# More gathered rows at the places of the second group's trunk, with three row buffers and whole weight blocks as they were

## The reference: what is computed

```python
x = x + merged @ w_mix_out       # the trunk: conv branch and GLA branch, gated and merged
x = x + _peer(_rmsnorm(x, norm2_g), peer_wq, peer_k1, peer_k2, peer_u, peer_v)
...
# in _peer, for each token: 8 heads of 16 experts each, of 16384
act = jax.nn.gelu(jnp.einsum('tkd,td->tk', u_tab[eb], hb))
return jnp.einsum('tk,tkd->td', gb * act, v_tab[eb])
```

## Time and profile before

| | |
|---|---|
| median of 3 runs | 4727.87 us (4722.62 to 4731.08) |
| the profiled execution | 4727.94 us, span 4725.9 us |
| PE busy | 4620.5 us (98%) |
| DVE busy | 2704.7 us (57%) |
| ACT, POOL busy | 542.8 us (11%), 904.6 us (19%) |
| data moved | 1352.17 MB, mean 286 GB/s |
| mean granted TensorE clock | 0.994 |

### The profile page before, as it was taken

The page is one execution under the profiler, slowest core; times in us unless marked ns, Lnnn a source line. Parts: engine busy times, 40 slices in busy tenths (PEclk is TensorE's granted clock), DMA queues, the critical chain, the costliest instruction groups (busy, mean ns, idle before and its releaser), DMA issues.

```text
span 4725.9 us, 47015 instructions
## 1 busy us (share of the span) xinstructions
PE 4620.5 (98%) x18646; PEld 3348.4 (71%) x18646; DVE 2704.7 (57%) x4672; ACT 542.8 (11%) x1255; POOL 904.6 (19%) x691
## 2 busy tenths in 40 slices
PE   8999999999999999999999999999999999999997
PEld 7888888888767567666667778888888844444443
DVE  4433500028567676645555459876878755555556
ACT  2111200011111101110000111112222200000000
POOL 1000000000111212023333232222333222222221
PEclk9999999999999999999999999999999999999999
DMA  4333444544667768568888789998998899999998
GB/s 176 142 136 140 159 152 145 209 177 154 215 229 256 298 222 308 200 234 347 350 338 352 278 342 341 342 332 330 359 348 333 335 395 412 412 383 411 417 411 326
DMA packets 239438, 1352.17 MB, mean 286 GB/s; under 512 B 43361, under 2 KB 43617, under 8 KB 133362
## 3 DMA queue, kind: packets, MB, share of 16 engines
q1 hardware_dynamic: 145362, 665.97, 37.9%
q0 software_dynamic: 93856, 683.19, 37.0%
HBM read 1308.38 MB, written 40.16 MB: 285 GB/s over the span
## 4 chain that ended last, share of the span: by engine, by line
PE 73%; DMA 19%; DVE 5%; issue 2%; ACT 0%; POOL 0%; POOLq 0%; DVEq 0%; ACTq 0%
PE ps L360 37%; PE ps L637 16%; PE ps L558 5%; PE ps L501 5%; DMA RING<-in_peer_v,table 4%; DMA RING<-in_peer_v,X 4%; DMA RING<-in_peer_u,X 4%; DMA RA<-in_uT 3%; DMA RING<-in_peer_u,table 3%; DVE CUR L857 2%; DVE RING L851 2%; PE pm L405 1%; PE ps L456 1%; PE pm L449 1%; PE ps L564 1%
## 5 line engine op out<-in xcount | busy, mean ns | idle before, releaser
L360 PE MATMUL ps<-X,BIG 128*128 128x320 f32 (+1 forms) x5632 | 1397.6, 410 | 6.9 <-DVE BIG L1242 6.4
L360 PEld LDWEIGHTS ps<-X,BIG 128*128 128x128 f32 x5632 | 1068.9, 190 | 319.0 <-issue 16.2
L857 DVE SCALAR_TENSOR_TENSOR CUR<-RING,wexp,CUR 128x2048 f32<-128x2048 f32 x320 | 752.0, 2350 | 398.2 <-DMA RING<-in_peer_v,table 283.4
L851 DVE CUSTOM_DVE_ANT_0 RING<-RING,CUR 128x2048 f32<-128x2048 f32 x320 | 730.3, 2289 | 405.5 <-DMA RING<-in_peer_u,table 276.0
L637 PE MATMUL ps<-X,RA 128*128 128x256 f32 x4096 | 903.6, 380 | 19.7 <-DMA RA<-in_uT 19.4
L637 PEld LDWEIGHTS ps<-X,RA 128*128 128x128 f32 x4096 | 773.4, 191 | 130.8 <-DMA RA<-in_uT 25.9
L1873 POOL DMA_INDIRECT RING<-in_peer_u,table x256 | 372.5, 1455 | 1364.0 <-DVE hidden L851 977.5
L1873 POOL DMA_INDIRECT RING<-in_peer_v,table x256 | 370.1, 1446 | 968.5 <-DVE CUR L857 754.6
L656 PE MATMUL ps<-RA,BIG 128*128 128x512 f32 x1024 | 492.2, 604 | 27.6 <-DMA RA<-in_peer_v 25.5
L656 PE MATMUL pm<-RA,BIG 128*128 128x512 f32 x1024 | 482.1, 594 | 1.3 <-DVE BIG L1352 1.3
L656 PEld LDWEIGHTS ps<-RA,BIG 128*128 128x128 f32 x1024 | 189.4, 191 | 295.2 <-issue 195.5
(11 more groups left out here) (293 smaller groups left out, 2886.4 us busy)
## 6 DMA issues: line engine op xcount, KB each, us to landing
BIG<-in_w_in_b SPq DMA_DIRECT2D x64, 2048.0 KB, 9.3
RA<-in_uT SPq DMA_DIRECT2D x256, 512.0 KB
RA<-in_peer_v SPq DMA_DIRECT2D x256, 512.0 KB
BIG<-in_w_gb_b SPq DMA_DIRECT2D x16, 2048.0 KB, 8.8
BIG<-in_w_ga_b SPq DMA_DIRECT2D x16, 2048.0 KB, 8.1
BIG<-in_w_gla_o_b SPq DMA_DIRECT2D x16, 2048.0 KB, 9.7
BIG<-in_w_mix_b SPq DMA_DIRECT2D x16, 2048.0 KB, 9.4
BIG<-in_w_q_b SPq DMA_DIRECT2D x16, 2048.0 KB, 9.1
```

The source lines that it names most:

```text
L360: last = pe.matmul(bank[:, 0:n], w[:, k, j * P:(j + 1) * P], src[:, k, 0:n], start=(k == 0), stop=(k == kt - 1))
L851: row_used.on(dve.tensor_tensor_reduce(out=row, in0=row, in1=h2cur[0:n, :], scale=1.0, scalar=0.0, op0=ALU.mult, op1=ALU.add, accum_out=hi ...
L857: row_used.on(dve.scalar_tensor_tensor(out=cur[0:n, :], in0=row, scalar=wexp[0:n, par, k:k + 1], in1=cur[0:n, :], op0=ALU.mult, op1=ALU.ad ...
```

## The change

Only numbers of the schedule change: how many gathered rows stand at each place of group 1's trunk.

```diff
-                    if g and tap in (5, 10, 15, 25):
+                    if g and tap in (3, 7, 11, 15, 25):
...
-                    spare((h, "z"), 4.8)
+                    spare((h, "z"), 7.2)
...
-                    spare((h, "kq"), 24.0)
+                    spare((h, "kq"), 28.8)
...
-                    spare((h, "conv"), 9.6)
+                    spare((h, "conv"), 12.0)
...
-                    spare((h, "r3"), 4.8)
+                    spare((h, "r3"), 7.2)
...
-                        spare((i, "mix"), 12.0 if i < D // PAIR - 2 else 0.0)
+                        spare((i, "mix"), 14.4 if i < D // PAIR - 2 else 0.0)
...
-                    spare((g, hd, "wq"), (13.0, 10.0)[g])
+                    spare((g, hd, "wq"), (13.0, 12.0)[g])
```

## The result

| | before | changed |
|---|---|---|
| median of the runs on one chip | 4729.48 us (4722.62 to 4731.88, 4 runs) | 4799.49 us (4796.40 to 4803.73, 4 runs) |
| profiled execution | span 4725.9 us, clock 0.994 | 4796.40 us, span 4794.4 us, clock 0.988 |
| ratio | | 1.0152, 95% interval 1.0139 to 1.0164 |

What follows compares the result with a forecast made beforehand. The prediction took the kernel as PE's time, plus some dense-pass waits and an end set by gathering. Its terms, 38.7 + 9.3 + 15 + 11 - 13 = +61 us on 4727.94, gave 4789 us, range 4742 to 4825.

Steps and rivals of the forecast that it cites:

- z and kq: Heads 1 to 3: added rows at 4.3 us delay DVE, so PE waits 38.7 us at the first v products.
- conv and taps: Heads: one row more at conv and one between the first taps cost PE 0, bounds 0 and 12 us.
- upper bound of 57 us: First v products: PE's wait if one row in each head waits as long as the fourth conv row.
- Rival B: Whole kernel: landing waits do not grow, r3 and mix fit their margins; +16, 4744 us; chance of 4737 to 4765: 0.22.
- the cheaper row of the Trainium skill: kq rows: about 358 GB/s from HBM gives 2.9 us a row, making the kq term 25 us.
- Clock: Behind three long waits at kq, PE returns at the lower level, losing 3.1 us each, 9.3 us more.
- Rival D: Whole kernel: a landing wait at every place, each bringing the lower clock; +115, 4843 us; chance of over 4825: 0.10.
- C: Whole kernel: the forecast itself, 4765 to 4825 us, likeliest 4789; chance 0.55.
- r3 and mix: r3: PE waits 3.7 us in each of four heads, 15 us; mix: six more rows make PE wait 11 us.
- Dense passes and end: u pass 0; gathering ends before PE in the v pass, end 11.6 us earlier plus 1.4 us, together -13.
- signs of being wrong: Changed profile: PE without gaps in the heads, kq rows closer together, or v pass shorter by more than the end.
- Rival A: Whole kernel: added rows replace DVE's waits, only the end changes; 4715 us, or 4700 if v-pass waits halve; chance 0.08.

Runs made afterwards that it cites:

- e5_owntime: The kernel before plus 4, 4 and 5 DVE additions that load nothing, behind the kq rows of heads 1 to 3; 4754.19 us, ratio 1.0058.
- e4_convtaps: The kernel before with only the conv and taps places as changed, 9 rows more before the u pass; 4725.27 us, ratio 0.9997.
- e2: The kernel before with only the r3 place as changed, 9 rows more before the u pass; 4729.16 us, ratio 1.0006.
- e8: The kernel before with 11 rows moved only to head 0's conv and taps and the mix's first three and seventh slots; 4702.29 us, ratio 0.9953.
- e6: The kernel before without the last 32 gathered rows, one of four heads of experts of the sample tokens not computed; 4707.27 us, ratio 0.9956.
- e1: The kernel before with only the z and kq places as changed, 13 rows more; 4756.58 us, ratio 1.0061.
- e3: The kernel before with only the mix as changed, 6 rows more; 4716.81 us, ratio 0.9985.
- e9_same: The kernel before again, unchanged, for a second profile; ratio 0.9997, given jointly with another unchanged repeat.

## Why the prediction was right, and where only by errors that cancel

The time was 10 us above the forecast, 72 us slower by the ratio where 61 was the sum. Its terms, for the profiled executions:

| term | forecast | measured |
|---|---|---|
| z and kq, waits at L501 | 38.7 | 40.2 |
| r3, waits at L456 | 15 | 13.8 |
| conv and taps | 0 (0 to 12) | 9.1 (15.6 alone) |
| slower products behind the waits of the heads | 9.3 | 23.0 |
| mix | 11 | 12.4 (8.9 of waits, 3.4 of slower products) |
| queries | 0 | 0 |
| u pass, v pass and end | -13 | -35 |

The 23.0 are the heads' 86.1 less the 63.1 us of waits in them; all but 0.3 us of it lie in the groups of products around the waits. The -35 is 1884.6 less the mean of the three profiles of before, 1919.3. The gates stay out, since 502.8 us lie within what the kernel before shows. The measured terms sum to 63.5 us, and the changed kernel's span is 64.8 us above the mean of the three.

So the mechanism was right, and the closeness of the total was in part luck: the losses in the trunk came out 24.5 us above their terms, and the gain behind it 22 us above its own.

*kq.* Right, in mechanism and size. The margins of the earlier trace rows and a price per row of 4.3 us (measured 3.97 to 4.56, mean 4.24) gave 38.7. Head by head it was less exact: 15.2, 14.2 and 10.8 against 13.2, 11.3 and 14.2. The upper bound of 57 us was mis-added: by the rows it names it is 55, or 61 if the row found in its buffer is the one that waits. Rival B, that only DVE's own time counts, falls with e5_owntime: that makes at most 25 of the 42 us. So does the cheaper row of the Trainium skill ("DMA: Bandwidth & Descriptors", "Where 436 GB/s comes from"): an estimate of 2.9 us a row from its figure would have given 25 us at L501, and the trace has 40.2.

*conv and taps.* "I put 0 on it" is the step that failed. I followed the rows only to the next product (the second v product at L1111), and there they did cost nothing (neither in the changed kernel nor in e4_convtaps does PE wait for L1111 or L1114). They are queued ahead of `silu_r` too, which had a margin of 0.6 us. Of the 23.8 us of e4_convtaps alone 15.6 are waits at L1046 and 2.4 at L501. Its products behind the L1046 waits are 8.6 us slower, and two other groups are 3.3 us faster than in the profile of before.

*Clock.* The term was counted for three waits and not for the four of L456 and the three of L1046, and its price, taken from one wait of 3.99 us in the u pass, was too high: 3.1 us a wait, against 2.3 on the mean of the ten (6.9 us at L501, 12.2 at L456, 3.8 at L1046). Rival D had the further waits for its case, and I left them out of C.

*r3 and mix.* Right in size: the fourth r3 row waited 3.43, 3.00, 3.00 and 2.83 us in heads 0 to 3 where I took 3.5. The mix's 11 us were meant as waits alone; these are 8.9, and the lower clock, not counted there either, makes up for it.

*Dense passes and end.* "-13" was too small by 22 us. I counted the end only as far as PE's end in the one profile, where PE was done 5 us before the sums. The repeats show that PE's end can come earlier and the kernel's does not follow: gathering sets the end in every profile of before, and the 21.5 to 30.5 us between PE's end and the span's shrink to 9.8. That is 12 to 21 us; the rest is shorter passes (u pass 960 against 966 to 973, v pass 914 against 916 to 928). From the u pass's start to PE's end it is 1874.8 us in the changed kernel and 1878.7 to 1879.3 in e2, e4 and e8, against 1886.6 to 1899.9 in the five profiles with no row moved (before three times, e5, e6). The other kernels with moved rows lie between, at 1881.0 to 1885.3, and e1 alone at 1891.7. So most of them have shorter passes than any kernel without, by some microseconds for which the forecast had nothing. One of its own signs of being wrong, a v pass that is shorter by more than the end, shows in the first pair of profiles: 13.3 us against 11.7. Against the repeats (916 and 920 us) it does not. The column "rest" says when this is won: 3 rows give 17 us, 6 give 23, 9 and 11 give 30, and 13 to 28 give 18 to 35. It does not grow with the rows beyond the first nine or so. Without this I could not have forecast that r3's 9 rows alone, with 23 us of loss, leave the time as it was.

*Rival A*, the rows are hidden, was wrong for this change but right for a smaller one: e8_free, with 11 rows in places of margin, is 0.5% faster, where A's 4715 us would be 0.3%.

Three kernels without a change to heads 1 to 3 (e3, e6, e8) end their heads at 1974.9 to 1976.3 us, where the three profiles of before have 1978.1 to 1980.4. Their traces say where: the first 128 products (L360) of a head take 34.56 us or, with no wait in them, 36.25 and once 37.53. The slower form stands in three heads of the first profile of before and two of each other one, in one of e3 and in none of e6 and e8. What decides it is open. Open stays too what shortens the u pass, and why 13 rows of e1 won less behind the heads than 9 rows of e2 (18 us against 31). For the last the profiles may say too much: e1's execution lay 3.7 us above its median and e2's 9 us below.

## What to carry to other kernels

Work that is put into an in-order engine's program has to be followed to every later instruction that another engine waits for, not to the first only; each has its own margin, and the smallest decides. A gain at the end saturates where the next bound takes over, while a loss in a stretch where the bounding engine has no slack adds row by row: move just so much as ends the last bound, into the places with measured margins. Take two more profiles of the kernel before to see which of its stretches are steady, and count every wait of TensorE with the slower products behind it, from the mean of several waits.

## What the runs showed of the hardware that was not expected

- The length of a wait alone does not tell whether TensorE comes back at the lower level. At the start of the gates PE has a wait of 2.15 us in all the profiles here, before the same products. Behind it 32 of them take 8.85 us in the first profile of the kernel before and 10.54 us in both repeats of the same program (rows below); of all fourteen profiles four have the fast form. In the changed kernel a wait of 2.63 us was followed by 10.54 us for 32 products and one of 3.60 us by 8.85. What tells the cases apart is open.
- A row's landing wait is no constant. The eleven kq rows of head 2 took 45.0 us in the kernel before and 49.6 us in e5_owntime, with up to 8.4 us before one row.
- The two passes together take PE 1886.6 to 1899.9 us in three executions of the same program, while the stretch to the end of the span differs by 4.3 us only, since gathering ends last.

The first row of the gates behind the wait, in the first profile of the kernel before and in e9_same:

```profile
2035.14 8.85 PE L360 MATMUL ps<-RA,BIG 128*128 128x320 f32 x32 [2.15 <-DVE RA L1224]
```
```profile
2034.16 10.54 PE L360 MATMUL ps<-RA,BIG 128*128 128x320 f32 x32 [2.15 <-DVE RA L1224]
```
